# A hybrid decoder step on one core: the second mixer's output projection in two passes, and the mLSTM heads two chunks behind

## What is computed

```python
for layer in range(2):
    h = rmsnorm(x, norm_mix[layer])
    if layer == 0:   # z = h @ w_in0; mLSTM heads (4 x 128) and pooling mixer (4 x 128)
        hm = head_norm(mlstm_scan(q, k, v, ig, lf, state)) * sigmoid(o)
        y = concat([hm, pool_mix(u, buf)]) @ w_out0
    else:            # latent attention; the samples attend to 4096 cached tokens in pages
        y = heads(mla_attend(...)) @ w_out1
    x = x + y
    x = x + relu(rmsnorm(x, norm_ffn[layer]) @ w_up[layer]) ** 2 @ w_down[layer]
y = rmsnorm(x, norm_final)
```

```python
s   = (q k^T) * w_intra                     # w_intra = exp(log_intra - m_t), causal
num = s v + w_inter * (C q)
h   = num / max(|sum(s) + w_inter * (n q)|, exp(-m_t))
C   = w_old * C + sum_s w_tok v k^T         # and n likewise
```

## Time and profile before

| | |
|---|---|
| median of 3 runs | 2836.72 us |
| profiled execution | 2837.73 us, its span 2835.9 us |
| mean granted TensorE clock | 0.973 |
| TensorE busy | 2694.7 us, 95% |
| VectorE, ScalarE, GpSimd busy | 36%, 21%, 28% |
| HBM | 58 GB/s over the span |
| chain that ended last | TensorE 76%, issue 16%, VectorE 4% |

### The profile page before, as it was taken

The page is one execution under the profiler, slowest core; times in us unless marked ns, Lnnn a source line. Parts: engine busy times, 40 slices in busy tenths (PEclk is TensorE's granted clock), DMA queues, the critical chain, the costliest instruction groups (busy, mean ns, idle before and its releaser), DMA issues.

```text
span 2835.9 us, 41068 instructions
## 1 busy us (share of the span) xinstructions
PE 2694.7 (95%) x16281; PEld 2380.6 (84%) x16281; DVE 1023.2 (36%) x2014; ACT 596.9 (21%) x1275; POOL 786.4 (28%) x432
## 2 busy tenths in 40 slices
PE   7999869999999999999999999796899999999998
PEld 4666556799999999999766667675899999999998
DVE  4111261432222222244544435354462222222224
ACT  3001451211100111021233333352220111001113
POOL 1003520333343334323000000331634333433340
PEclk9999889999999999999999999998999999999999
DMA  3113311211111111111000000883211111111101
GB/s 107 37 38 107 113 34 28 66 48 50 45 44 47 49 44 44 45 51 34 10 29 19 19 0 0 287 275 108 60 45 45 46 51 44 44 46 50 44 30 60
DMA packets 186039, 166.41 MB, mean 59 GB/s; under 512 B 15972, under 2 KB 174950, under 8 KB 181645
## 3 DMA queue, kind: packets, MB, share of 16 engines
q1 hardware_dynamic: 167806, 113.24, 13.5%
q0 software_dynamic: 7584, 41.98, 4.2%
q10 hardware_dynamic: 10551, 9.83, 1.1%
HBM read 155.88 MB, written 9.36 MB: 58 GB/s over the span
## 4 chain that ended last, share of the span: by engine, by line
PE 76%; issue 16%; DVE 4%; SPq 1%; ACT 1%; DMA 1%; POOL 0%; POOLq 0%; DVEq 0%; ACTq 0%
PE psum L1837 25%; PE psum L1853 25%; PE psum L496 14%; PE psum L1879 5%; PE psum L2041 2%; SPq L519 1%; PE psum L2053 1%; PE psum L2076 1%; DVE Zr L1633 1%; DVE Zr L442 0%; DMA Z<-in_x_sample 0%; PE psum L2057 0%; POOLq L370 0%; PE psum L1807 0%; DVE M L451 0%
## 5 line engine op out<-in xcount | busy, mean ns | idle before, releaser
L1411 DVE TENSOR_TENSOR x<-psum,x 128x344 f32<-128x344 f32 x384 | 197.7, 516 | 472.6 <-PE psum L1853 472.6
L1837 PE MATMUL psum<-Gr,Mr 128*128 128x344 f32 x1536 | 367.7, 321 | 0.0
L1853 PE MATMUL psum<-Zr 128*128 128x344 f32 x2304 | 365.9, 320 | 1.2 <-DVE x L1411 1.2
L1853 PE MATMUL psum<-Zr,Mr 128*128 128x344 f32 x2304 | 365.7, 320 | 0.0
L1837 PE MATMUL psum<-Gr,Zr 128*128 128x344 f32 x1536 | 365.4, 320 | 0.0
L1853 PEld LDWEIGHTS psum<-Zr 128*128 128x128 f32 x2304 | 363.4, 188 | 1.5 <-DVE x L1411 1.5
L1853 PEld LDWEIGHTS psum<-Zr,Mr 128*128 128x128 f32 x2304 | 363.5, 188 | 0.0
L966 ACT ACTIVATE Zr<-M 128x344 fp32r<-128x344 f32 x192 | 94.4, 492 | 1181.4 <-DVE M L1399 1181.4
L496 PE MATMUL psum<-G,W 128*128 128x344 f32 (+1 forms) x1008 | 298.8, 458 | 8.6 <-DVE G L377 6.5
L733 POOL TENSOR_TENSOR Zr<-W,ones 128x1024 fp32r<-128x1024 f32 x75 | 145.3, 1937 | 546.5 <-PE psum L1853 232.8
L733 POOL TENSOR_TENSOR Mr<-W,ones 128x1024 fp32r<-128x1024 f32 x68 | 131.8, 1939 | 593.8 <-PE psum L1837 216.0
(11 more groups left out here) (345 smaller groups left out, 3164.0 us busy)
## 6 DMA issues: line engine op xcount, KB each, us to landing
W<-in_w_up SPq DMA_DIRECT2D x64, 512.0 KB, 4.1
W<-in_w_down SPq DMA_DIRECT2D x64, 512.0 KB, 3.4
W<-in_w_in SPq DMA_DIRECT2D x26, 512.0 KB, 4.0
W<-in_w_out SPq DMA_DIRECT2D x16, 512.0 KB, 4.0
Z<-in_x_prompt SPq DMA_DIRECT2D x8, 512.0 KB, 7.2
M<-kq_scratch ACTq DMA_DIRECT2D x8, 512.0 KB, 4.4
out_y_p<-Z SPq DMA_DIRECT2D x8, 512.0 KB
M<-decay_scratch SPq DMA_DIRECT2D x6, 512.0 KB, 3.4
```

Of the source, the lines that this page charges most:

```text
L1411: dve.tensor_tensor(x[:, m, blk(b)], bank[v % DBANKS][:, 0:TB], x[:, m, blk(b)], ALU.add)\
L1837: mm = pe.matmul(bank[v % DBANKS][:, 0:TB], w[:, k, :], r[:, k, blk(b)], start=(k == 0 and c == 0), stop=(k == KD - 1 and c == 2))
L1853: mm = pe.matmul(bank[v % DBANKS][:, 0:TB], w[:, k, :], r[:, k, blk(b)], start=(k == 0 and c == 0), stop=(k == KH - 1 and c == 2))
```

## The change

Projection of the second mixer. Its units run in the order `RES1`: blocks 0 and 1 of all panels, then block 2 of all panels, starting with those four whose weights are still split. Four panels are loaded and split a second time (12 in all, ring `RING1`). High and low halves of blocks 0 and 1 are made before the merge; VectorE's merge and its evictions are interleaved; own scores stand behind unit 0, the transposes ahead of unit 7, the values ahead of unit 8. The barrier is gone. The merge's operands are moved to other places and to PSUM banks 4 to 7. The finishing of the projection has its own functions, with 688 columns at a time in the first pass.

Scan. All last decays are computed ahead (`dall`); `dlast` and its semaphore are gone. ScalarE copies the numerators to SBUF (`raw`); statistics and scaling read that copy. The state comes first in VectorE's chunk, the heads one chunk later than before. The samples' own heads move in front of the scan, the pooling matmuls into its tail, and the first broadcast loads ahead of the last output gate.

```diff
+ORDER1 = [(KD // 2 + j) % KD for j in range(KD)]
+RES1 = [(m, b) for m in range(KD) for b in range(NB - 1)] + [(m, NB - 1) for m in ORDER1]
+RING1 = (0, 1, 0, 1, 0, 1, 2, 3, 0, 1, 2, 3)
+FIN1 = [(m, slice(0, (NB - 1) * TB)) for m in range(KD)] + [(m, slice((NB - 1) * TB, T)) for m in ORDER1]
...
+        def low1(dve, j):
+            k, at = FIN1[j]
+            dve.wait_ge(sem("fin_gh"), 2 * FIN + j + 1)
+            dve.scalar_tensor_tensor(out=gxl[1][:, k, at], in0=x[:, k, at], scalar=gain(VROW["norm_ffn"] + KD + k),
+                                     in1=gxh[:, k, at].bitcast(F32), op0=ALU.mult, op1=ALU.subtract).then_inc(sem("fin_gl"), 1)
...
             def decays(n, s, i):
                 pool.wait_ge(sem(f"bc_in{s}"), i * 16 + 16)
-                wait(pool, "ml_state", n - 1)
-                pool.tensor_tensor(dlast[s], bc[s][:, :, 1, CH - 1], ones[:, 0:H], ALU.mult).then_inc(sem("ml_last"), 1)
                 wait(pool, "ml_num", n - 1)
...
                         if layer == 1:
-                            pool.wait_ge(sem("dense_mm"), U_OUT1 + (NB * (j + 5) if j < 2 else KD * NB))
+                            pool.wait_ge(sem("dense_mm"), U_OUT1 + (NB - 1) * KD + KD // 2 + j + 1)
...
-            phase_end(pool, 5)
-            split_dense(OUT1, MLP1 - OUT1, wsp[1], S_OUT1, U_OUT1)
+            pool.wait_ge(sem("sa_pv"), NS * NQ)
+            for j in range(MLP1 - OUT1):
+                pool.wait_ge(sem(f"w_in{(OUT1 + j) % SLOTS}"), arrived[OUT1 + j])
+                if 2 <= j < 6:
+                    pool.wait_ge(sem("dense_mm"), U_OUT1 + (NB - 1) * (j - 1))
+                if j == 6:
+                    pool.wait_ge(sem("self_mm"), 3)
+                if j >= KD:
+                    pool.wait_ge(sem("dense_mm"), U_OUT1 + (NB - 1) * KD + j - KD + 1)
+                split(OUT1 + j, wsp[1][RING1[j]], S_OUT1 + j)
...
             # ScalarE, scan
+            def raw(n, s):
+                act.wait_ge(sem("ml_num"), n + 1)
+                wait(act, "ml_ap", n - 1)
+                act.copy(hraw[s]..., psum[:, 3 * 512:5 * 512]...).then_inc(sem("ml_raw"), 1)
             def chunk(n, s):
-                    deviation(n - 1)
+                    raw(n - 1, 1 - s)
                     exponentials(n + 1, 1 - s)
                     weighted_keys(n + 1, 1 - s)
+                    deviation(n - 1)
                     stage(n + 2)
...
             # VectorE, scan
+                if n >= 1:
+                    new_state(n - 1, 1 - s)
+                if n >= 2:
+                    heads(n - 2)
+                if n >= 1:
+                    denominators(n - 1)
+                if n + 1 < NC:
+                    weigh(n + 1, 1 - s)
+                if n + 2 < NC:
+                    columns(n + 2, s)
+                if n >= 1:
+                    normalised(n - 1)
...
             # VectorE, projection: pass one ends with evict1(15)
+            for v in range(9, len(RES1)):
+                evict1(v)
+                if 9 <= v < 15:
+                    total1(dve, v - 8)
+                if v == 16:
+                    total1(dve, KD - 1)
+                    low1(dve, 0)
+                if 17 <= v < 23:
+                    low1(dve, v - 16)
+                if v > 17:
+                    total1(dve, v - 9)
+            low1(dve, KD - 1)
+            for j in range(KD, 2 * KD - 2):
+                low1(dve, j)
+            total1(dve, 2 * KD - 1)
+            for j in range(2 * KD - 2, 2 * KD):
+                low1(dve, j)
...
             # TensorE, scan
                 products(n, s)
+                numerators(n, s)
                 if not isinstance(n, int) or n >= 1:
                     head_transposes(n - 1)
-                numerators(n, s)
...
             # TensorE, projection
+            def output_unit(v):
+                m, b = RES1[v]
+                if b == 0:
+                    pe.wait_ge(sem("mlp_split"), S_OUT1 + m + 1)
+                if b == NB - 1 and m < KD // 2:
+                    pe.wait_ge(sem("mlp_split"), S_OUT1 + KD + m + 1)
+                if v < NB - 1 or v == (NB - 1) * KD:
+                    pe.wait_ge(sem("o_lo"), b + 1)
+                if v >= DBANKS:
+                    pe.wait_ge(sem("dense_ev"), U_OUT1 + v - DBANKS + 1)
...
+            for v in range(len(RES1)):
+                if v == 1:
+                    own_scores()
+                if v == 7:
+                    merged_transposes()
+                if v == 8:
+                    sample_values()
+                output_unit(v)
```

More of the change, by code:

```diff
@@ L191, in build @@
         C1 = tg(H, P + 1)
+        hraw = [tg(H, P + 1) for _ in range(2)]
         tm = carve(M)
@@ L887, in _ @@
             sample_store(NS - 1)
[L888 to L893, removed]
             phase_end(act, 2)
@@ L1096, in _, with outputs_high @@
             weights(NS * NQ - 1)
+            def outputs_high(b):
+                act.copy(oh[:, :, blk(b)], oT[:, :, blk(b)]).then_inc(sem("o_hi"), 1)
+            act.wait_ge(sem("sa_pv"), NS * NQ - 2)
+            for b in range(NB - 1):
+                outputs_high(b)
             act.wait_ge(sem("self_in"), 6)
@@ L1099, in _ @@
             act.activation(wself, sself, ACT.Exp, bias=oneg).then_inc(sem("sc_exp"), 1)
[L1100 to L1103, removed]
+            act.wait_ge(sem("self_in"), 9)
+            outputs_high(NB - 1)
+            finish_scalar1(act)
             norm_roots(act, 3)
@@ L1318, in normalised @@
                 for h in range(H):
-                    two, at = half(h)
-                    w = dve.tensor_scalar(hn[:, h, :], bank[3 + two][:, at.start:at.start + P], mv[:, h, 0:1], hsc[:, h:h + 1],
+                    w = dve.tensor_scalar(hn[:, h, :], hraw[n % 2][:, h, 0:P], mv[:, h, 0:1], hsc[:, h:h + 1],
                                           ALU.subtract, ALU.mult)
@@ L1786, in _, with pooled @@
                 chunk(NC - 2 + s, s)
+            def pooled(units):
+                for j in units:
+                    g, b = divmod(j, NB)
+                    if j >= 2:
+                        pe.wait_ge(sem("pm_ev"), j - 1)
+                    pe.matmul(bank[1 + j % 2][:, 0:TB], wpool[:, g, :], ups[:, g, blk(b)], start=True, stop=True)\
+                      .then_inc(sem("pm_mm"), 1)
+            pe.wait_ge(sem("pool_in"), 32)
+            pe.wait_ge(sem("ml_kw"), NC)
+            pe.wait_ge(sem("ml_vtok"), NC)
+            pooled(range(0, 6))
             head_transposes(NC - 1)
-            pe.wait_ge(sem("sh_v"), 1)
-            pe.transpose(bank[0][0:HC, 0:P], svp, ident).then_inc(sem("sh_t"), 1)
+            pooled(range(6, 9))
             pe.wait_ge(sem("ml_state"), NC)
@@ L2090, in _ @@
                     page_values(n - 2)
-            pe.wait_ge(sem("self_in"), 5)
-            own = bank[0][0:R, 0:1]
-            for r in range(2):
-                pe.matmul(own, prodc[:, r, :, :].rearrange("p b h -> p (b h)"), ones[:, 0:1], start=(r == 0), stop=False)
-            pe.matmul(own, prodp.rearrange("p b h -> p (b h)"), ones[0:ROPE, 0:1], start=False, stop=True)
-            for r in range(2):
-                mm = pe.transpose(bank[1][0:R, r * P:(r + 1) * P], ckb[:, r, :, :].rearrange("p b h -> p (b h)"), ident)
```

238 lines of the change are left out of this document (141 added, 97 removed).

## The result

The changed kernel takes 2815.98 us (median of 4 runs, 2815.15 to 2818.07) against 2836.77 for the kernel before (2836.35 to 2837.07, 4 runs beside it): ratio 0.9928, 95% interval 0.9911 to 0.9945. The forecast was 2818.5, faster. The time is right, but three of its four terms are not: the scan step's had the wrong sign, the tail's was half of what came, the projection's about 0.6 of it. The profiled spans, 2835.9 and 2813.4, are 22.5 us apart, 1.7 more than the medians.

The account below looks back on a forecast made before the run. TensorE, busy 95% of the span, was taken as the bound except in the sample merge and mLSTM scan. Savings of 8.7 + 4.6 + 1.3 + 3.6 = 18.2 us from the median 2836.7 gave 2818.5 us; range 2804 to 2831.

Parts of the forecast that it names:

- scan step: mLSTM scan: 8.4 us a chunk instead of 9.06, 58.8 for seven, so 4.6 us saved; bounds 7.4 and 10.7.
- tail: From the last numerators to the first output projection: 18.5 us against 22.1, so 3.6 us saved; bounds 16.5 and 23.
- projection: Second mixer's projection up to the MLP's start: 8.7 us saved in all, out of 30 gained at its start.
- Projection, start: After the last page product: unit 0 waits only for the first split panel and low half, starting 30 us earlier.
- Inline work: Returns among the projection's units: own scores 1.1 us, transposes 0.5, values 3.5, waits of 2 and 4.5, clock 3.6.
- Pass two: Projection's end: VectorE and GpSimd instructions take turns, last sum at 2089.2 instead of 2097.9, leaving 8.7 us of 30.
- rival D: Scan: each normalisation waits for one GpSimd mask of 1.27 us, 8.9 later than forecast, 2827.4 us; chance 0.07.
- F: Slower: TensorE at half clock wherever it has gaps, 10.7 us a scan chunk, 2842.7 us in all; chance 0.06.
- Start: Scan's beginning: decay broadcast issued before the last gate, exponentials' table load at 340.9 instead of 342.2; 1.3 us saved.
- low halves of 2.5 us or more in pass two: Sign in the projection: VectorE's low halves of 688 columns slowed to 2.5 us or more each by GpSimd.
- a wait of 5 to 12 in the first MLP units: Sign at the MLP's start: TensorE waits 5 to 12 us there, unless VectorE keeps up.
- head transposes that wait for the scaled heads: Sign in the scan: TensorE's head transposes stand waiting for VectorE's normalised heads; no size given.

Follow-up runs that it names:

- experiment 6: Changed kernel with ScalarE instead of GpSimd making the high halves of the eight panels split in pass two; 2807.24 us, ratio 0.9899 to the kernel before.
- experiment 5: Changed kernel with useless identity products filling TensorE's gap before the scaled heads in the scan; 2818.1 us with twenty, 2810.13 us with twelve.
- Experiment 7: Changed kernel with all twelve pooling products issued behind the last head transposes and the state's transposes; 2817.85 us, ratio 0.9935 to the kernel before.
- experiments 3: Changed kernel with TensorE's scan written out chunk by chunk instead of in a loop, in the same order; 2818.48 us, ratio 0.9935 to the kernel before.

## Why the prediction was right, and where it was wrong

**Projection, start: right.** Unit 0 was forecast 7.3 us behind the last page product and came 7.14 behind. **Inline work: right**, a little too dear: own scores waited 1.69 (2), the merge's transposes 2.95 (4.5), its steps took 15.2 with one eviction between (17 from first to last was counted), the two half-clock units lost 3.6 (3.6). Unit 16 ended 84.4 us behind the page's end; 86.9 was forecast.

**Pass two: the mechanism right, the size off.** The alternation was there in every pair, and experiment 6 shows that it set the MLP's start. From unit 16's end to the sum over partitions it was 44.8, where 47.6 was forecast: GpSimd's 16 instructions took 40.9 with VectorE's between them (43.3), and the rest 3.9 (4.3). With the 2.5 from before this makes the 14.0 of the table against 8.7. The kernel after has the shortest stretch of the eight profiles that share this version of it; they give 11.6 to 14.0 saved, so of the 5.3 missing at least 2.9 is the forecast's error.

**Scan step: wrong.** The step that failed is "So 8.4 a chunk: 58.8 for seven". At full clock the loop is 8.65 (experiment 5), and without the blocked scaling, 0.9 less, it would be 7.75 (no run has both in this order), near the sum of durations that I made (7.9). The order of the loop was right too. Two terms were mis-sized. The scaling was bounded by 1.0 and 1.37 and measured 2.02: I had cited the very rule by which it would stand behind GpSimd and put it into rival D, with 0.07, because no row showed it. (D named the mask, 1.27 a step; it was the weighing of the queries behind the mask, and 0.9.) And the half clock was priced at 0.5 by the mean clock of the old scan; it cost 1.5, since here the gap of 3.6 comes in every step and the slow instructions all lie in the loop. So the five middle steps took some 10.15: 8.4, 0.9 more for the scaling, 1.0 more for the clock, and 0.15 less for the sum of durations. Rivals D and F described what happened there. F said that it decides from a step of 9.9 on; the step passed that and the kernel was faster all the same. Two things were wrong in F's sum. It took seven such steps, where the first and the last are short in the new order. And it added 4.5 for the tail and the values, where the tail saved 7.1 and the projection 14.0: even seven steps of 10.15 would have left the kernel some 15 us faster.

**Tail: the size off, by an error in the working.** I added the last heads (6.3) and the twelve pooling units one behind the other; the changed kernel issues six of them ahead. Experiment 7 puts them behind and measures 20.1, near the 18.5 of that sum; with the overlap it is 15.0. The slow clock that it priced at 2 showed in three or four units, 1.0 to 1.15 us apart where 0.75 is the pace at full clock. **Start:** 1.9 against 1.3, but the first numerators lie between 344.8 and 349.8 in the kernels with this start, so the profile of one run doesn't measure this term, and no experiment isolates it. Where they came 2 to 4.6 earlier and the order was the same (experiments 3 and 7), the first step was longer, 11.3 and 11.6, so such an early start was in part given back.

The total was 2.5 us off by luck, not by the working. The errors in the profile were -5.3 (step), +3.5 (tail), +5.3 (projection) and +0.6 (start), 4.1 in all. The stretches with a forecast of 0 add 0.2, and 1.8 goes off because the profiled execution before lies 1.0 above its median and the one after 0.8 below. The range held for the same reason.

**What the prediction named as signs:** low halves of 2.5 us or more in pass two, seen in seven of eight (2.56 to 3.05, one 2.13); a wait of 5 to 12 in the first MLP units, 8.7 seen; head transposes that wait for the scaled heads, seen; table loads every 8 to 8.5, not seen (10.1 to 10.3), which by its own words makes that part wrong.

## What to carry to other kernels

When an order is changed, write down the new loop in the order of each engine's queue, and see whether an instruction that waits for the loop's end stands ahead of the one that begins the next turn; moving four transposes behind the next scores was worth more (12.0 in scan and tail) than the whole scan edit (8.3 in start, scan and tail). A TensorE gap inside a loop is priced by what runs right behind it, not by the mean clock of the stretch. And count VectorE's instructions with two SBUF inputs (or a scaling from SBUF) against GpSimd's one by one: if they cannot alternate within a unit, and ScalarE has room, give it half of GpSimd's.

## What the runs showed of the hardware

Filling a gap with 12 useless products made the granted clock of the scan 1.00 instead of 0.83, and the scan 8.7 us shorter from first to last numerators (57.2 against 65.9). Gaps of 3.5 to 3.9 us were followed by half clock in each of five steps; behind gaps of 2.7 to 3.0 the first four transposes ran at full clock every time, though twice the scores after them did not. The length of the gap alone does not tell: in the kernel before, of two gaps of 2.3 ahead of the scores one was followed by half clock (2.07 for the eight) and one was not (1.16). A scaling of four times 128 columns takes 1.37 us from PSUM, beside GpSimd's mask too. From SBUF it takes 1.11 with GpSimd idle, but 2.0 when a GpSimd instruction has begun 0.1 us before it: the faster source is the slower one beside GpSimd.
